# The scaling of the attention exponentials on GpSimd: one column as a second tensor in place of a number per partition

## The chip, the core and the metric

The kernel runs on one core of a Trainium2 chip. The metric is the device time of one execution in microseconds. Five engines take part: TensorE (PE in the profile; its weight loads PEld), VectorE (DVE), ScalarE (ACT), GpSimd (POOL) and SyncE (SP), which issues the DMAs. They run side by side and wait for each other by semaphores.

## What is computed

The program is a network of two blocks with two layers each, for 512 tokens of width 1024, with 256 context tokens beside them in the second block. The change lies in the attention of the second block's last layer:

```python
def gqa_sdpa(q, k, v):
    B, Q, H, Dh = q.shape
    qg = q.reshape(B, Q, N_KV_HEADS, KV_GROUP, Dh)
    s = jnp.einsum("bqkgd,bskd->bkgqs", qg, k).astype(jnp.float32) * (Dh ** -0.5)
    p = jax.nn.softmax(s, axis=-1).astype(v.dtype)
    o = jnp.einsum("bkgqs,bskd->bqkgd", p, v)
    return o.reshape(B, Q, H * Dh)
```

There are 16 heads of 64 and 4 heads of keys and values; 512 queries look at 512 + 256 = 768 keys. Behind the attention come its output product (wo), a norm and a gated feed-forward layer.

## The kernel before, in words

The attention is the function `gqa_attend` on TensorE, with loops over the same tiles on the other engines. A tile is one head and 128 queries, so there are 64 tiles n = 0 to 63, four to a head. Each tile goes through these steps:

- TensorE, `scores` (L1004, L1005): four matmuls write 128x768 scores into one of two pairs of PSUM banks. They wait for L2263 of tile n - 2.
- VectorE, L1802: reduction to the negative maximum.
- ScalarE, L2263: exponential into p2 (five buffers, 128x768 fp32 in SBUF), with the sum of each row in rs2. For an odd tile it also waits for the transposes of tile n - 5 and of the tile before that.
- VectorE, L1814: reciprocal of the sum into ri2, one column of a small tile.
- GpSimd, L2355: p2 = p2 x ri2, in place. This is the line that changes.
- TensorE, `turn`: transposes of p2 (L1015 four blocks of a tile, L1022 the two context blocks of both tiles of a pair, after the odd one).
- ScalarE, L2271 and L2275: the high part of the transposes; VectorE, L1819 and L1823: the low part.
- TensorE, `pv` (L1035, L1036): 12 matmuls for a pair of tiles, into the head's half of the PSUM bank of y2. All heads use the one bank of the ring "mod"; the first pair of a head waits until the head before is out of it.
- ScalarE, L2283, moves one half of y2 to SBUF (stat_t); VectorE, L1809, adds both halves into y2_out and frees the bank.
- For every second head ScalarE, L2287, and VectorE, L1828, split y2_out into a high and a low part in q_parts, which the output product reads. L1828 is the one large operation of VectorE here with two SBUF inputs.

Each engine works through its queue in the order in which it is written. In step n TensorE runs scores of n, then for even n the PV product of the pair (n - 8, n - 7), then the transposes of n - 4. VectorE runs in step n: L1802 of n; L1809 where n mod 4 is 3 (of head (n - 11)/4); L1814 of n - 1; L1819 of n - 5; L1823 for even n; L1828 where n mod 8 is 1. ScalarE runs L2263 of n, L2271 of n - 4, L2275 for odd n, and L2283 where n mod 4 is 2. GpSimd has nothing but L2355 in this stage, and waits before each for L1814 of the tile. Earlier in the program GpSimd takes the low parts of half of the weights (L2310, a subtraction with two full tensor inputs) and builds the weights of a convolution (L2327, a product whose second input repeats each value 32 times by a step of zero); in the attention TensorE's products need no weights from DMA.

Names: `sum_inverse` is the signal of L1814, `p2_scaled` that of L2355. P is 128, SEQ 512, CTX 256.

Of the kernel before, what the change touches and what calls it, by code (L numbers as in the profile page):

```python
# [17 lines left out]
ALU = mybir.AluOpType  # L18
# [6 lines left out]
P = 128  # L25
# [6 lines left out]
class Tally:  # L32
# [17 lines left out]
    def mark(self, name, *event, by=1):  # L50
        self.raised[name] = self.raised.get(name, 0) + by
        assert (name, event) not in self.at, (name, event)
        self.at[name, event] = self.raised[name]
        return self.sems[name], by

    def ready(self, name, *event):
        if self.known is None:
            return self.sems[name], self.at.get((name, event), 1)
        return self.sems[name], self.known[name, event]
# [34 lines left out]
def write(nc, a, out, tally):  # L94

    mark, ready = tally.mark, tally.ready
    _, SEQ, D = a["x"].shape
    CTX = a["ctx_2"].shape[1]
    DEPTH = a["w_in"].shape[0]
# [90 lines left out]
    def vec(name, i=0, n=1):  # L190
        c = vec_at[name] + i
        return vcols[:, c:c + n]

    def const(name, lo=0, n=None):
        c, w = CST[name]
        return cst[:, c + lo:c + (w if n is None else lo + n)]
# [76 lines left out]
    p2 = [nc.alloc_sbuf_tensor_at(f"p2{i}", [P, SEQ + CTX], F32, offset=int(hl_base + 8 * KB + 3 * KB * i)) for i in range(2)]  # L273
# [4 lines left out]
    ri2 = [small[:, 40 + i:41 + i] for i in range(5)]  # L278
# [15 lines left out]
    for row, n, src, dup in vec_rows:  # L294
        while n:
# [8 lines left out]
            row, n = row + k, n - k  # L304
# [13 lines left out]
    def full(job):  # L318
        return ready("bank_full%d" % bank_of[job], *job)

    def free(job):
        return tally.sems["bank_free%d" % bank_of[job]], use_of[job]
# [47 lines left out]
    def by_pool(key):  # L370

        return key[0] in BLOCK_1_SLABS or key[0:2] == ("dn", 1)
# [12 lines left out]
    def _(pe):  # L385
# [78 lines left out]
        def linear_pair_both(tag, *two):  # L464

            c_tag = (*tag[:-1], "c")
            hc = h_of(c_tag)
            tally.h_before[tag] = tally.h_before[c_tag] = tally.h_reader[0]
            ws = []
            for job, src, kind in two:  # L470
                begin(job, "pair")
                ws.append(slab(job, k_p(src), KD, src.shape[1], kind))
            tally.h_reader[0] = two[1][0]
            for s, t in (("x", tag), ("c", c_tag)):
                for i in range(KD):
                    pe.wait_ge(*ready("h_low", t, i))
                    for (job, _, _), w in zip(two, ws):
                        mm = both(job, w, i, slice(0, P), (Hh[:, i, :], Hl[:, i, :]), (hc[0][:, i, :], hc[1][:, i, :]),
                                  i == 0, i == KD - 1, s)
                        if s == "c" and i == KD - 1:  # L480
                            mm.then_inc(*fill(job))
                            release[job] = full(job)

        def linear_pair(tag, n, *two):

            tally.h_before[tag] = tally.h_reader[0]
            ws = []
            for job, src, kind in two:
                begin(job)
                ws.append(slab(job, k_p(src), KD, src.shape[1], kind))  # L490
            tally.h_reader[0] = two[1][0]
            for i in range(KD):
                pe.wait_ge(*ready("h_low", tag, i))
                for (job, _, _), w in zip(two, ws):
                    mm = three(bank(job, n), w[0][:, i, :], w[1][:, i, :], Hh[:, i, 0:n], Hl[:, i, 0:n],
                               i == 0, i == KD - 1)
                    if i == KD - 1:
                        mm.then_inc(*fill(job))
                        release[job] = full(job)
            mods()  # L500
            mods()
# [643 lines left out]
    def halves(slab, src, dst):  # L1145

        _, _, k, w, kind = slab
        if kind != "twice":
            return src[:, 0:k * w], dst[:, 0:k * w]
        return (src[:, 0:k * w].rearrange("p (k c) -> p k c", k=k).unsqueeze(2).broadcast_to([P, k, 2, w]),  # L1150
                dst[:, 0:2 * k * w].rearrange("p (k e c) -> p k e c", k=k, e=2))
# [1148 lines left out]
    @block.gpsimd  # L2300
    def _(pool):
        for i, (o, src) in enumerate(pieces[1]):
            pool.dma_start(o, src).then_inc(*mark("vec_in_rest", *([i] if i + 1 < len(pieces[1]) else []), by=16))
        for d, one in enumerate(slabs):
            if not by_pool(one[0]):
                break
            src, high = halves(one, raw[d % RAW], Wh[d % WS])
            _, low = halves(one, raw[d % RAW], Wl[d % WS])
            pool.wait_ge(*ready("w_high", one[0]))
            pool.tensor_tensor(low, src, high.bitcast(F32), ALU.subtract).then_inc(*mark("w_low_pool", one[0]))  # L2310


        w_dw = vec("w_dw", 0, TAPS * KD).rearrange("p (t j) -> p t j", j=KD)
        pool.wait_ge(*ready("w_low_pool", slabs[d - 1][0]))
        for g in range(4):
            for i in range(4):
                one = pool.tensor_copy(tap_cols[32 * i:32 * i + 32, g, :, :],
                                       w_dw[32 * g:32 * g + 32, PE_FIRST + i:PE_FIRST + i + 4 * QUADS - 3:4, :])
                one.then_inc(*mark("tap_cols", g, i))
                pool.wait_ge(*ready("tap_cols", g, i))  # L2320
        pool.wait_ge(*full(("dn", 1, DEPTH - 1, "x", 1, KD - 1)))
        for j in range(KD):
            if j >= 2:
                pool.wait_ge(*full(("taps", j - 2)))
            w = tap_cols[:, :, :, j].rearrange("p g q -> p q g").unsqueeze(3).broadcast_to([P, QUADS, 4, 32])
            fold = const("fold").unsqueeze(1).unsqueeze(1).broadcast_to([P, QUADS, 4, 32])
            pool.tensor_tensor(WQ[j % 2][:, :, :, :], fold, w, ALU.mult).then_inc(*mark("tap_weights", j))  # L2327

        def own(inst, *event):
            inst.then_inc(*mark("ctx_parts", *event))  # L2330
            return ready("ctx_parts", *event)

        pool.wait_ge(*ready("x_new", ("ffn", 0, "x"), KD - 1))
        pool.wait_ge(*ready("head_scaled", "k2", "c", KVH // 2 - 1))
        pool.wait_ge(*free(("turned", "v2", "c", 1)))
        for e in range(2):
            at_e = slice(e * HD, (e + 1) * HD)
            src = k_ctx[at_e, 0:KVH // 2, :]
            for d in range(2):
                pool.wait_ge(*own(pool.tensor_copy(k_hi[d * HD:(d + 1) * HD, e::2, SEQ:], src), "k", e, d))  # L2340
            for d in range(2):
                low = pool.tensor_tensor(k_lo[d * HD:(d + 1) * HD, e::2, SEQ:], src, k_hi[at_e, e::2, SEQ:].bitcast(F32),
                                         ALU.subtract)
                pool.wait_ge(*own(low, "k_low", e, d))
        for c in range(2):
            v = v_ctx[:, :, c * P:(c + 1) * P].rearrange("p t (g d) -> p t g d", g=2)
            one = v_parts[:, QT:, 2 * c:2 * c + 2, :, :]
            for b in (0, 2):
                pool.wait_ge(*own(pool.tensor_copy(one[:, :, :, b, :], v), "v", c, b))
            i = pool.tensor_tensor(one[:, :, :, 1, :], v, one[:, :, :, 0, :].bitcast(F32), ALU.subtract)  # L2350
        own(i)
        for n in range(G_HEADS * QT):
            h, i = divmod(n, QT)
            pool.wait_ge(*ready("sum_inverse", n))
            pool.tensor_scalar(p2[n % 5][:, :], p2[n % 5][:, :], ri2[n % 5], None, ALU.mult)\  # L2355
                .then_inc(*mark("p2_scaled", h, i))

    @block.sync
# [111 lines left out]
```

## Time and profile before

| | us |
|---|---|
| median of 3 runs | 3382.73 |
| lowest, highest | 3376.64, 3382.94 |
| the profiled execution | 3380.34 |
| its span, first to last instruction | 3378.5 |
| TensorE busy | 3250.6 (96%) |
| VectorE busy | 1484.0 (44%) |
| ScalarE busy | 1189.3 (35%) |
| GpSimd busy | 764.8 (23%) |

The mean granted clock of TensorE is 0.987 of full speed, and 1.00 in nearly all of the attention stage. The stage runs from about 2771 to 2919 us of the span. The shares are means over the whole program: GpSimd's 23% says nothing of the one stage in which it works without a pause. Matmuls are pipelined and the end of each is modelled, so times of TensorE are best read from start to start. A group in the list of groups gives busy time, mean length of one and the idle time before them, with what ended it.

### The profile page before, as it was taken

The numbers are of one execution on the slowest core, as the hardware profiler recorded it, in microseconds if no ns is written. First come the engines' busy times: TensorE is split into PE (matmuls) and PEld (weight loads), VectorE is DVE, ScalarE is ACT, GpSimd is POOL, SyncE is SP. The second block draws the span as 40 slices with busy tenths as digits, with TensorE's granted clock in tenths as the row PEclk, the third lists the DMA queues.
The fourth block names the chain that finished last, engine by engine and source line by source line (L and its number), as shares of the span: only waits on it lengthen the run. The fifth ranks groups of instructions, "written<-read, shape, count | busy, mean of one in ns | idle before, by whom it ended". The sixth has DMA issues, their size and how long they took to land.

```text
span 3378.5 us, 39102 instructions
## 1 busy us (share of the span) xinstructions
PE 3250.6 (96%) x15860; PEld 2490.3 (74%) x15860; DVE 1484.0 (44%) x2110; ACT 1189.3 (35%) x1752; POOL 764.8 (23%) x399
## 2 busy tenths in 40 slices
PE   6999999999998999999999899999999879999998
PEld 4657777777665776777777576888888648868886
DVE  3562143132356114313369746222334889653234
ACT  3433234233343323423331154111112558632222
POOL 4302433443330333434311000000000039500000
PEclk9999999999999999999999999999999989999999
DMA  6403434444440355455435311222221110123322
GB/s 231 139 26 94 150 118 149 151 142 151 124 126 19 117 158 168 149 188 161 133 88 128 83 47 39 65 63 64 68 63 57 38 38 1 38 69 89 104 85 72
DMA packets 429894, 337.25 MB, mean 100 GB/s; under 512 B 16637, under 2 KB 411223, under 8 KB 417428
## 3 DMA queue, kind: packets, MB, share of 16 engines
q1 hardware_dynamic: 428272, 334.23, 32.7%
q8 instruction: 127, 2.08, 0.3%
q0 software_dynamic: 1248, 0.46, 0.1%
q14 instruction: 51, 0.42, 0.0%
q10 hardware_dynamic: 196, 0.07, 0.0%
HBM read 319.58 MB, written 2.10 MB: 95 GB/s over the span
## 4 chain that ended last, share of the span: by engine, by line
PE 85%; DVE 6%; POOL 4%; ACT 2%; issue 1%; SPq 1%; DMA 0%; POOLq 0%; DVEq 0%; ACTq 0%
PE PS L422 25%; PE PS L423 24%; PE PS L424 24%; POOL p L2355 4%; PE PS L585 3%; PE PS L511 2%; PE PS L735 1%; PE PS L890 1%; PE PS L564 1%; PE PS L924 1%; SPq L2380 1%; DVE both_tmp L1260 1%; PE PS L943 1%; PE PS L901 1%; PE PS L923 1%
## 5 line engine op out<-in xcount | busy, mean ns | idle before, releaser
L422 PE MATMUL PS<-Hh,Wh 128*128 128x512 f32 x2208 | 876.9, 397 | 13.8 <-DVE Hl L1274 9.6
L423 PE MATMUL PS<-Hl,Wh 128*128 128x512 f32 x2208 | 862.8, 391 | 0.0
L424 PE MATMUL PS<-Hh,Wl 128*128 128x512 f32 x2208 | 862.3, 391 | 0.0
L2310 POOL TENSOR_TENSOR Wl<-raw,Wh 128x1024 fp32r<-128x1024 f32 (+2 forms) x254 | 568.3, 2242 | 1119.4 <-ACT Wh L1861 1119.4
L1861 ACT ACTIVATE Wh<-raw 128x1024 fp32r<-128x1024 f32 (+2 forms) x442 | 435.9, 987 | 402.9 <-PE PS L424 394.3
L422 PEld LDWEIGHTS PS<-Hh,Wh 128*128 128x128 f32 x2208 | 416.1, 188 | 138.2 <-issue 73.5
L424 PEld LDWEIGHTS PS<-Hh,Wl 128*128 128x128 f32 x2208 | 416.2, 189 | 87.8
L423 PEld LDWEIGHTS PS<-Hl,Wh 128*128 128x128 f32 x2208 | 416.3, 189 | 67.3 <-issue 3.1
L1183 DVE TENSOR_TENSOR Wl<-raw,Wh 128x1024 fp32r<-128x1024 f32 (+3 forms) x188 | 217.6, 1158 | 385.8 <-ACT Wh L1861 385.4
L1764 DVE SCALAR_TENSOR_TENSOR cv<-PS,vcols,cv 128x510 f32<-128x510 f32 (+1 forms) x176 | 123.7, 744 | 296.2 <-ACT cv L2231 296.2
L422 PE MATMUL PS<-g_h,Wh 128*128 128x512 f32 x528 | 210.6, 399 | 0.0
L423 PE MATMUL PS<-g_l,Wh 128*128 128x512 f32 x528 | 208.6, 395 | 0.0
L424 PE MATMUL PS<-g_h,Wl 128*128 128x512 f32 x528 | 208.5, 395 | 0.0
L2340 POOL CAST k_hi<-k_ctx 64x512 fp32r<-64x512 f32 x4 | 3.6, 912 | 815.4 <-DVE k_ctx L1260 815.2
L422 PE MATMUL PS<-hc_h,Wh 128*128 128x256 f32 x576 | 163.1, 283 | 1.0 <-DVE hc_l L1274 0.9
L423 PE MATMUL PS<-hc_l,Wh 128*128 128x256 f32 x576 | 161.9, 281 | 0.0
L424 PE MATMUL PS<-hc_h,Wl 128*128 128x256 f32 x576 | 161.8, 281 | 0.0
L2355 POOL TENSOR_SCALAR p<-p,small 128x768 f32<-128x768 f32 x64 | 141.7, 2237 | 56.2 <-DVE small L1814 56.2
L1738 DVE SCALAR_TENSOR_TENSOR X<-PS,mod,X 128x512 f32<-128x512 f32 x48 | 36.0, 751 | 261.0 <-PE PS L424 261.0
L511 PE MATMUL PS<-sq,cst 128*128 128x512 f32 (+2 forms) x244 | 114.4, 587 | 32.6 <-ACT sq L1896 13.6
L2231 ACT ACTIVATE cv<-PS,vcols 128x512 f32<-128x512 f32 x88 | 68.5, 778 | 211.7 <-PE PS L424 210.2
L422 PEld LDWEIGHTS PS<-g_h,Wh 128*128 128x128 f32 x528 | 99.1, 188 | 37.8 <-issue 14.7
(357 smaller groups left out, 4863.8 us busy)
## 6 DMA issues: line engine op xcount, KB each, us to landing
raw<-in_ffn_w SPq DMA_DIRECT2D x108, 512.0 KB, 3.7
mod_w<-in_w_mod SPq DMA_DIRECT2D x48, 1024.0 KB, 5.4
raw<-in_w_up SPq DMA_DIRECT2D x88, 512.0 KB, 3.8
mod_w<-in_w_ada SPq DMA_DIRECT2D x40, 1024.0 KB, 5.9
raw<-in_w_in SPq DMA_DIRECT2D x62, 512.0 KB, 4.1
UQ<-U SPq DMA_DIRECT2D x128, 99.4 KB, 2.2
raw<-in_w_down SPq DMA_DIRECT2D x32, 384.0 KB, 3.4
raw<-in_conv_w_pw SPq DMA_DIRECT2D x24, 512.0 KB, 4.5
```

What stands on the lines that cost most here:

```text
L422: pe.matmul(o, wh, xh, start=start, stop=False, skip_group_check=True)
L423: pe.matmul(o, wh, xl, start=False, stop=False, skip_group_check=True)
L424: return pe.matmul(o, wl, xh, start=False, stop=stop, skip_group_check=True)
L511: mm = pe.matmul(bank(job, n), const(matrix)[lo:hi, :], SQ[i][lo:hi, 0:n], start=first, stop=final, skip_group_check=True)
L585: mm = pe.matmul(PS[32 * j:32 * j + b, bank_of[job], :], cact[b][:, r, :], w[:, 512 * j:512 * (j + 1)], start=r == 0, stop=r == KD - 1, sk ...
L1183: dve.tensor_tensor(low, src, high.bitcast(F32), ALU.subtract).then_inc(*mark("w_low", k))
L1738: dve.scalar_tensor_tensor(X[:, j, :], bank(job), g, X[:, j, :], ALU.mult, ALU.add).then_inc(*empty(job))
L1764: ins = dve.scalar_tensor_tensor(o, bank(ups[s])[:, 0:SEQ - lag], vec(("w_conv", l), tap * 2 * FC + s * FC + f), o, ALU.mult, ALU.add)
L1861: act.activation(high, src, ACT.Copy).then_inc(*mark("w_high", k))
L2231: act.activation(cv[f % 2][s][:, :], bank(job), ACT.Identity, bias=vec(("b_conv", l), s * FC + f), scale=vec(("w_conv", l), 2 * 2 * FC + s ...
L2310: pool.tensor_tensor(low, src, high.bitcast(F32), ALU.subtract).then_inc(*mark("w_low_pool", one[0]))
L2355: pool.tensor_scalar(p2[n % 5][:, :], p2[n % 5][:, :], ri2[n % 5], None, ALU.mult)\
```

## The change

```diff
         for n in range(G_HEADS * QT):
             h, i = divmod(n, QT)
             pool.wait_ge(*ready("sum_inverse", n))
-            pool.tensor_scalar(p2[n % 5][:, :], p2[n % 5][:, :], ri2[n % 5], None, ALU.mult)\
+            pool.tensor_tensor(p2[n % 5][:, :], p2[n % 5][:, :], ri2[n % 5].broadcast_to([P, SEQ + CTX]), ALU.mult)\
                 .then_inc(*mark("p2_scaled", h, i))
```

GpSimd's 64 products take the reciprocal sums no longer as a number per partition but as a second tensor operand: the same column with a step of zero, read once for each of the 768 elements of a row. What is computed, the buffers, the waits and the order of all queues stay as they are.

## Rows read from the trace of the kernel before

**Rows 1.** The page: the span, and the chain that ended last.
```profile
span 3378.5 us, 39102 instructions
...
PE 85%; DVE 6%; POOL 4%; ACT 2%; issue 1%; SPq 1%; DMA 0%; POOLq 0%; DVEq 0%; ACTq 0%
```

**Rows 2.** The chain in order of time, 2760 to 2930: start, us, what.
```profile
2775.56 135.12 POOL p L2355 x61
```

**Rows 3.** A window amid the stage: length, busy PE, PEld, DVE, ACT, POOL, clock, DMA.
```profile
2820.00:2840.00 20.00, 19.55 (x147) 17.58 (x147) 19.24 (x37) 17.15 (x36) 20.00 (x10) 1.00 0.00 1
```

**Rows 4.** Waits from 2785 to 2905: who for whom, us in total, times, longest.
```profile
PE PS L1015 <- POOL p L2355: 2.2, 6, 0.4
PEld PS L1035 <- DVE y_out L1809: 1.7, 6, 0.3
```

**Rows 5.** Line L2355: duration in ns, shortest, median, longest, and where.
```profile
L2355 POOL TENSOR_SCALAR p<-p,small x64: 2198/2207/2535, 2772.9 to 2912.8; 128x768 f32<-128x768 f32 x64
```

**Rows 6.** Groups of GpSimd's instructions by shape: busy us, mean ns, idle before.
```profile
L2310 POOL TENSOR_TENSOR Wl<-raw,Wh 128x768 fp32r<-128x768 f32 x36 | 66.3, 1843 | 131.3 <-ACT Wh L1861 131.3
```

**Rows 7.** Instructions in time, GpSimd's L2327, then one of VectorE: start, us, what.
```profile
1718.08 2.13 POOL L2327 TENSOR_TENSOR WQ<-cst,tap_cols 128x512 f32<-128x512 f32 x2 [4.63 <-PE PS L424]
...
1795.86 2.63 POOL L2327 TENSOR_TENSOR WQ<-cst,tap_cols 128x512 f32<-128x512 f32 x1 [20.66 <-PE PS L735]
...
2805.89 0.68 DVE L1828 TENSOR_TENSOR q_parts<-y_out,q_parts 128x512 fp32r<-128x512 f32 x1
```

**Rows 8.** TensorE in order of time, amid the stage.
```profile
2792.61 0.36 PE L1035 MATMUL PS<-pt_hi,v_parts 128*128 128x256 f32 x1
...
2799.41 0.28 PE L1005 MATMUL PS<-k_lo,q_parts 128*128 128x256 f32 x1
...
2801.47 0.39 PE L1035 MATMUL PS<-pt_hi,v_parts 128*128 128x256 f32 x1
...
2802.99 0.60 PE L1015 MATMUL PS<-cst,p 128*128 128x128 f32 x4
2803.34 0.47 PE L1004 MATMUL PS<-k_hi,q_parts 128*128 128x512 f32 x1
...
2805.70 0.28 PE L1035 MATMUL PS<-pt_hi,v_parts 128*128 128x256 f32 x1
...
2808.14 0.28 PE L1005 MATMUL PS<-k_lo,q_parts 128*128 128x256 f32 x1
...
2810.39 0.33 PE L1035 MATMUL PS<-pt_hi,v_parts 128*128 128x256 f32 x1
```

**Rows 9.** VectorE in order of time, the same stretch.
```profile
2799.73 0.96 DVE L1802 TENSOR_REDUCE small<-PS 128x1 f32<-128x768 f32 x1 [0.35 <-PE PS L1005]
2800.72 0.69 DVE L1809 TENSOR_TENSOR y_out<-PS,stat_t 64x512 f32<-64x512 f32 x1
...
2803.18 0.67 DVE L1819 TENSOR_TENSOR pt_lo<-PS,pt_hi 128x512 fp32r<-128x512 f32 x1
2803.77 0.68 DVE L1823 TENSOR_TENSOR pt_lo<-PS,pt_hi 128x512 fp32r<-128x512 f32 x1
...
2808.61 0.94 DVE L1802 TENSOR_REDUCE small<-PS 128x1 f32<-128x768 f32 x1
2809.60 0.68 DVE L1809 TENSOR_TENSOR y_out<-PS,stat_t 64x512 f32<-64x512 f32 x1
```

**Rows 10.** The stage's end: four rows of TensorE, then one of VectorE.
```profile
2908.20 0.39 PE L1035 MATMUL PS<-pt_hi,v_parts 128*128 128x256 f32 x1 [0.68 <-DVE y_out L1809]
...
2909.73 0.60 PE L1015 MATMUL PS<-cst,p 128*128 128x128 f32 x4
2910.82 0.63 PE L1015 MATMUL PS<-cst,p 128*128 128x128 f32 x4 [0.49 <-POOL p L2355]
...
2917.92 0.35 PE L1035 MATMUL PS<-pt_hi,v_parts 128*128 128x256 f32 x1 [0.25 <-DVE pt_lo L1823]
...
2915.03 0.68 DVE L1809 TENSOR_TENSOR y_out<-PS,stat_t 64x512 f32<-64x512 f32 x1 [1.54 <-ACT stat_t L2283]
```

## The prediction

> **What bounds the kernel now.** I read the page first. The span is 3378.5 us, and the time of this execution is 3380.34, so 1.84 us lie outside it; sums below are made on 3380.34. The chain of work that ended last is 85% TensorE and 4% GpSimd, and those 4% are one line, L2355, the one that changes [rows 1]. In order of time, that share is one unbroken piece: GpSimd carries the chain from 2775.56 for 135.12 us, all of it the scaling of the exponentials in the last attention [rows 2]. So the change touches 64 instructions in one stage of about 147 us, and that stage's end decides, since the gemm behind it starts as soon as it ends.
>
> That GpSimd is the bound there is only half of the story. In the middle of the stage GpSimd is busy all of 20 us, but TensorE 19.55 and VectorE 19.24 [rows 3]. Three engines run nearly full, so a faster GpSimd gives only what lies between its pace and the next. The waits say which is next: from 2785 to 2905 TensorE waited 2.2 us for the scaling, and 1.7 us in six places for VectorE's addition L1809 to release a PSUM bank [rows 4].
>
> **What the change costs by itself.** Removed: 64 TENSOR_SCALAR of 128x768, shortest 2198 ns, median 2207 [rows 5]. Added: 64 TENSOR_TENSOR of 128x768, whose second input is one column, with step zero. Waits, signals, buffers and the order on each queue stay the same. The trace of before has no TENSOR_TENSOR with a one-column input of this length, so I bound it. With two full inputs and the same width GpSimd takes 1843 ns [rows 6]. Nearest with a step of zero is L2327 (512 wide; one input repeats each value 32 times): two of them take 2.13 us together, so about 1.07 each; alongside dense VectorE work on two SBUF tensors it takes 2.63 [rows 7]. Scaled by width these are 1.07 x 1.5 = 1.60 and 2.63 x 1.5 = 3.95. I take 1.84: same width, same memory, two inputs. The 3.95 is an end for the bad case only, because in this stage VectorE's big operations read PSUM and at most one SBUF tensor; only L1828, eight times, reads two. One of those starts at 2805.89 [rows 7] in the middle of a scaling; the longest scaling, 2535 ns, is the mark of it [rows 5], +0.33 us.
>
> The Trainium skill ("GPSIMD Engine Reference", section 4.1) says that two-input elementwise operations are about 2x slower on GpSimd than on VectorE while one-input ones run roughly at line rate; by that the swap would be a loss. The trace says otherwise: the one-input form takes 2207 ns for 768, the two-input form 1843. The Trainium skill's own figure for a two-input add (the same page, section 3.1, 4497 ns for 2048 elements) would make 768 an estimated 1.69 us; the sum below would not move by it.
>
> **What is late next.** GpSimd alone would save 64 x (2.21 - 1.84) = 24 us. It can't, since another circuit closes almost as tightly. The PV products of all heads (4 tiles each) share one PSUM bank, which L1809 frees. L1809 stands on VectorE's queue right behind a reduction L1802; that reduction waits for its tile's scores; those scores stand on TensorE's queue behind the first PV product of the head that holds the bank now; and the next head's first PV product waits for this L1809. Step by step, from rows in which no wait for GpSimd lies:
> - TensorE from L1035 at 2801.47 to the last score matmul at 2808.14: 6.67 us [rows 8] (two PV products, three groups of scores, and the transposes between).
> - last score matmul to the reduction: 2799.41 to 2799.73, 0.32 us where VectorE is free; 2808.14 to 2808.61, 0.47, where it is still busy with the L1828 of that head pair [rows 8, 9].
> - reduction to L1809: 2799.73 to 2800.72, and 2808.61 to 2809.60: 0.99 both times; L1809 itself 0.69; its end to L1035 0.06 (2801.41 to 2801.47) [rows 8, 9].
> Sum: 6.67 + 0.32 + 0.99 + 0.69 + 0.06 = 8.73 us for four tiles. Every second head has L1828, and there VectorE has no gap at all from L1809 at 2800.72 to L1809 at 2809.60, 8.88 us [rows 9]; with L1809 and 0.06 behind it that gives the next L1035 at 2810.34, where it now stands at 2810.39 [rows 8]: 8.87. The pair costs 8.73 + 8.87 = 17.60 us.
>
> Today: from L1035 at 2792.61 to L1035 at 2908.20 are 13 intervals, 115.59 us, mean 8.89 [rows 8, 10]. The kind with L1828 (2801.47 to 2810.39) is 8.92, the other kind (115.59 - 6 x 8.92) / 7 = 8.87, by the rows one by one 8.86. So the gain in the steady part is 7 x (8.86 - 8.73) + 6 x (8.92 - 8.87) = 0.9 + 0.3 = **1.2 us**. Before 2792.61 nothing is gained: that first L1035 already waits for an L1809 (its own reduction waits for TensorE, not for GpSimd).
>
> The drain. GpSimd is two tiles behind there, and that backlog vanishes. Transposes 61 start at 2910.82 after a wait for GpSimd; they follow the group at 2909.73, and such a group holds TensorE 0.35 (2802.99 to 2803.34 [rows 8]), so they could start at 2910.08, 0.74 earlier. Everything to L1809 at 2915.03 (PV, transposes 62, ScalarE's copy) moves with them, to 2914.29. The scaling of tile 63 no longer queues behind others and is done well before. Then VectorE runs L1809, two L1819 and L1823 back to back, 0.59 apart (2803.18 to 2803.77 [rows 9]), the last one for its 0.68, and TensorE takes it up about 0.15 later: 2914.29 + 3 x 0.59 + 0.68 + 0.15 = 2916.9 for the last L1035, now 2917.92 [rows 10]: **1.0 us**. Behind it TensorE runs the same gemms, shifted.
>
> Sum: 3380.34 - 1.2 - 1.0 = 3378.1, say **3378.0 us**, 0.07% less. The median of the runs shown, 3382.73, is 2.4 us above the profiled one; from there it would be 3380.5. A change of under 0.2% (6.8 us) can hardly be told from none with runs that spread over 6.3 us.
>
> The GpSimd price doesn't enter this, as long as it stays under the circuit: eight scalings and one +0.33 must fit in 17.60, so up to (17.60 - 0.33) / 8 = 2.16 us. Both 1.60 and 1.84 give the same time. That is the cover, and it is thin on the other side: from 2.16 up each 0.1 us costs 6.4.
>
> **The rivals.**
> - The circuit is looser than I think (L1809 follows its reduction sooner, as VectorE catches up), and TensorE's own work sets the pace. From L1035 at 2801.47 to the next tile pair's at 2805.70 are 4.23 us [rows 8], 4.13 without the 0.10 by which the waiting L1035 runs long, so 8.26 for four tiles: 13 x (8.89 - 8.26) + 1.0 = 9.2 us gained: 3371.1. Against it: 0.99 stands at both places shown, and waits of L1035 for L1809 exist already [rows 4]. Chance 0.10.
> - The other side: the one-column input is slow. If the same column read 768 times costs what L2327 costs beside a busy VectorE, 3.95 us, GpSimd sets the pace: 63 x (3.95 - 2.21) = 110 us more, 3490. It decides from 2.16 us; at 2.54 (the longest scaling today) it is 63 x 0.33 = 21 us, 3401. Against it: L2327 with a step of zero takes 1.07 when it is left alone. Chance 0.06. The Trainium skill's rule above, taken at its word (section 4.1, a one-input form at twice the rate), would end here too: an estimated 4.4 us each and some 3519.
> - L1828 gets blocked behind a scaling. Six of the eight lie in the tight heads; each blocked for a whole 1.84 us is 11 us more on VectorE's unbroken chain, net 3389. Against it: L1828 takes 0.68 while a scaling runs [rows 7], as long as L1809 and L1819 of the same width [rows 9]; GpSimd stretches instead. Chance 0.03. "SBUF — State Buffer", section "SBUF: two separate sides", of the Trainium skill calls the shared port pair an exclusive lock for the whole instruction, whoever starts first; in the trace VectorE isn't held.
> - The change doesn't do what it says: the instruction ends up as the same one, 2.207 us. 3380.3. Chance 0.04.
>
> **How the numbers follow.** Forecast 0.77, the rivals 0.10, 0.06, 0.03, 0.04. Faster by over 0.2%: the looser circuit, 0.10. Slower by over 0.2%: 0.09. Within 0.2%: 0.77 + 0.04 = 0.81. The forecast's own range: the steady part can give between nothing and twice my 1.2, the drain between nothing and 1.0, and the runs shown lie 3.7 below to 2.6 above the profiled one; that makes 3373 to 3383. Widened to take in most of the looser circuit and the low end of the blocked L1828: **3370 to 3386**.
>
> **What would show it.** L2355 as TENSOR_TENSOR, at 1.6 to 1.85 us, and GpSimd idle before each one, waiting for L1814; its share in the chain gone from 4% to nearly nothing, DVE and PE in its place. L1035 waiting for L1809 in 13 places instead of 6 or 7, with intervals of 8.73 and 8.87. TensorE no longer waiting for GpSimd. The stage ending 2 us sooner. It would be wrong if L2355 took over 2.16 us, if the intervals fell well under 8.7, or if L1802, L1819 or L1828 grew longer beside the new operation.

## The result

The changed kernel takes 3387.95 us (median of 12 runs, 3383.65 to 3388.92); the kernel before takes 3382.2 in 12 runs beside it. The ratio is 1.0018, with a 95% interval of 1.0010 to 1.0027: slower by 3 to 9 us. The forecast was 3378.0, in a range of 3370 to 3386. The measured time lies above the range. What turned the gain of the attention stage into a loss is one of the forecast's own rivals, which it had given a chance of 0.03; that accounts for some 5 of the 10 us of the miss, and the section on the prediction says what the rest is.

The page of the kernel after: the span, the chain that ended last by engine, and then, from the list of GpSimd's groups by shape, the line that was changed.

```profile
span 3387.1 us, 39102 instructions
...
PE 87%; DVE 7%; ACT 2%; issue 2%; SPq 1%; DMA 0%; DVEq 0%; ACTq 0%
...
L2355 POOL TENSOR_TENSOR p<-p,small 128x768 f32<-128x768 f32 x64 | 93.8, 1468 | 104.5 <-DVE small L1814 103.2
```

GpSimd has left the chain altogether (4% in [rows 1]), its scaling is 0.74 us shorter than before (1468 ns against a median of 2207 [rows 5]), and it now stands idle for 104.5 us waiting for reciprocals, 55.7 of them before its first scaling (before the change 56.2 in all). Two thirds of the old price, and the kernel is slower. The waits of the kernel after from 2771 to 2930, longest in total first:

```profile
POOL p L2355 <- DVE small L1814: 103.2, 45, 55.7
...
PEld PS L1035 <- DVE y_out L1809: 9.1, 15, 1.1
```

TensorE's wait for L1809 is the one that grew: from 2771 to 2918 in the kernel before it was 2.6 us in 7 places. Where it comes from shows in VectorE's queue around the line L1828, then GpSimd's at the same time (start, us, what):

```profile
2810.45 0.67 DVE L1819 TENSOR_TENSOR pt_lo<-PS,pt_hi 128x512 fp32r<-128x512 f32 x1
2811.04 1.59 DVE L1828 TENSOR_TENSOR q_parts<-y_out,q_parts 128x512 fp32r<-128x512 f32 x1
2812.55 0.94 DVE L1802 TENSOR_REDUCE small<-PS 128x1 f32<-128x768 f32 x1
...
2810.61 1.47 POOL L2355 TENSOR_TENSOR p<-p,small 128x768 f32<-128x768 f32 x1 [0.65 <-DVE small L1814]
```

L1828 takes 1.59 us; before it took 0.68 [rows 7]. It starts 0.43 us after a scaling has started and ends 0.55 after that scaling's end (2810.61 + 1.47 = 2812.08): it was held. Over all eight of its instances in the kernel after, shortest, median, longest:

```profile
L1828 DVE TENSOR_TENSOR q_parts<-y_out,q_parts x8: 681/1586/1592, 2811.0 to 2930.1; 128x512 fp32r<-128x512 f32 x8
```

Six take 1.59 us. The last two, at 2921.05 and 2930.07, start when no scaling is under way and take 0.68 and 0.69.

The first PV products of the heads, TensorE in order of time, give the pace:

```profile
2797.89 0.38 PE L1035 MATMUL PS<-pt_hi,v_parts 128*128 128x256 f32 x1
...
2806.61 0.38 PE L1035 MATMUL PS<-pt_hi,v_parts 128*128 128x256 f32 x1 [0.20 <-DVE y_out L1809]
...
2816.40 0.39 PE L1035 MATMUL PS<-pt_hi,v_parts 128*128 128x256 f32 x1 [0.23 <-DVE y_out L1809]
...
2825.14 0.39 PE L1035 MATMUL PS<-pt_hi,v_parts 128*128 128x256 f32 x1 [0.20 <-DVE y_out L1809]
...
2917.66 0.39 PE L1035 MATMUL PS<-pt_hi,v_parts 128*128 128x256 f32 x1 [0.90 <-DVE y_out L1809]
...
2926.41 0.35 PE L1035 MATMUL PS<-pt_hi,v_parts 128*128 128x256 f32 x1 [0.20 <-DVE pt_lo L1823]
...
2927.85 0.39 PE L422 MATMUL PS<-q_parts,Wh 128*128 128x512 f32 x1
```

Intervals are 8.72, 9.79, 8.74 and so on in turn. Heads without L1828 run at the forecast 8.73 (8.86 before); heads with it at 9.79 (8.92 before, 8.87 forecast). From 2797.89 to 2917.66 are 119.77 us, before 115.59 [rows 8, 10]: 4.2 lost. From there to the first gemm behind are 10.19, before 11.20 (2908.20 to 2919.40): 1.0 won, as forecast. The stage costs 130.0 us in place of 126.8, **3.2 us more**.

The two profiled spans differ by 8.6 us, and 5.3 of these lie before the stage: L1035 at 2792.61 [rows 8] is L1035 at 2797.89 here. The change touches nothing there: the first scores of the stage (L1004) start at 2763.72 before and at 2769.01 now, 5.29 apart. What differs is where TensorE's granted clock was at its lower level (1.2 GHz for 3 to 17 us at a time, else 2.4). Two windows, from 220 to 235 and from 1050 to 1065 us, in the kernel before and then in the kernel after (length, busy PE, PEld, DVE, ACT, POOL, clock, DMA):

```profile
220.00:235.00 15.00, 11.37 (x51) 8.02 (x51) 8.84 (x11) 7.37 (x6) 0.00 (x0) 1.00 0.00 1
...
1050.00:1065.00 15.00, 11.37 (x42) 7.55 (x41) 9.46 (x11) 5.92 (x6) 0.00 (x0) 0.77 0.00 1
```

```profile
220.00:235.00 15.00, 11.37 (x42) 7.69 (x41) 8.66 (x9) 6.89 (x6) 0.00 (x0) 0.77 0.01 1
...
1050.00:1065.00 15.00, 11.37 (x54) 7.95 (x53) 10.58 (x13) 7.47 (x8) 0.00 (x0) 1.00 0.01 1
```

The same matmuls meet another clock, and not always to the loss of the same kernel. Up to the first scores the lower level lasted 69.9 us in all in the kernel before and 83.5 in the kernel after. ScalarE's instructions, matched between the two traces, show the lag grow by some 2.8 us after the low stretch at 224 and by 1.5 after the one at 914, and shrink by 2.8 where only the kernel before has one, at 1055. A comparison of two spans alone would have put 8.6 us down to the change; stages must be compared with stages.

### The profile page after: what moved, and what is told of

Its sections match the earlier page's. It is cut to its first block, busy times and chain, and to the rows that moved or that the text cites. A ratio compares the mean times of both kernels' runs of the same rounds, so it can differ in the third digit from the quotient of the medians.

```text
span 3387.1 us, 39102 instructions
## 1 busy us (share of the span) xinstructions
PE 3254.4 (96%) x15860; PEld 2491.2 (74%) x15860; DVE 1488.5 (44%) x2110; ACT 1189.9 (35%) x1752; POOL 717.4 (21%) x399
## 4 chain that ended last, share of the span: by engine, by line
PE 87%; DVE 7%; ACT 2%; issue 2%; SPq 1%; DMA 0%; DVEq 0%; ACTq 0%
PE PS L422 25%; PE PS L423 24%; PE PS L424 24%; PE PS L585 3%; PE PS L511 2%; PE PS L735 1%; PE PS L890 1%; PE PS L564 1%; PE PS L924 1%; SPq L2380 1%; DVE both_tmp L1260 1%; PE PS L943 1%; DVE small L1802 1%; PE PS L901 1%; PE PS L923 1%
## 5 line engine op out<-in xcount | busy, mean ns | idle before, releaser
L1183 DVE TENSOR_TENSOR Wl<-raw,Wh 128x1024 fp32r<-128x1024 f32 (+3 forms) x188 | 217.6, 1158 | 386.1 <-ACT Wh L1861 385.6
L422 PEld LDWEIGHTS PS<-hc_h,Wh 128*128 128x128 f32 x576 | 108.1, 188 | 23.8 <-DVE hc_l L1312 1.9
```

Of the source, the lines that this page charges most:

```text
L422: pe.matmul(o, wh, xh, start=start, stop=False, skip_group_check=True)
L1183: dve.tensor_tensor(low, src, high.bitcast(F32), ALU.subtract).then_inc(*mark("w_low", k))
```

## The experiments

All lengths of the stage below are from the first PV product of the second head (the row at 2792.61 in [rows 8]) to the first gemm behind the attention.

| kernel | scaling | stage, us | median, us (runs) | ratio to before |
|---|---|---|---|---|
| before | number | 126.8 | 3382.2 (12) | |
| changed | column | 130.0 | 3387.95 (12) | 1.0018 [1.0010, 1.0027] |
| again | column | 130.0 | 3387.93 (11) | 1.0016 [1.0007, 1.0025] |
| after_move | column | 125.3 | 3378.67 (11) | 0.9993 [0.9984, 1.0001] |
| before_move | number | 125.5 | 3383.0 (11) | 1.0003 [0.9994, 1.0011] |
| full2 | full tensor | 132.4 | 3389.72 (6) | 1.0025 [1.0014, 1.0036] |
| full2_move | full tensor | 125.7 | 3382.82 (10) | 1.0000 [0.9991, 1.0009] |
| yadd_first | column | 136.6 | 3395.37 (4) | 1.0043 [1.0027, 1.0058] |
| copy_first | column | 128.9 | 3384.89 (11) | 1.0007 [0.9998, 1.0016] |
| ts_copy_first | number | 129.2 | 3385.64 (11) | 1.0013 [1.0004, 1.0022] |
| pv_late | column | 134.1 | 3393.78 (5) | 1.0035 [1.0021, 1.0048] |
| ts_pv_late | number | 134.2 | 3393.09 (11) | 1.0029 [1.0020, 1.0037] |

The ratios are to the executions of the kernel before that ran beside each, with medians of 3381.5 to 3382.3.

The mean granted clock of an execution, from 0.985 to 0.989 on record, goes with the time whatever the kernel: a straight line with the same slope for each kernel, through the 174 executions of this table and of the kernel before beside them, gives an estimated 2.4 us for each 0.001. At equal clock the changed kernel (23 executions) lies 4.3 us above before (71), give or take 0.6 (95%); after_move lies 0.6 below and before_move 0.1 above, both give or take 0.8. The medians of the table mix such executions: seven of 71 of the kernel before had 0.988 or more, none of the 23 of the changed kernel, and four of the 11 of after_move.

### Is it the stage, always?

> The changed kernel as it is, once more, to see what of the 8.6 us between the two profiled spans belongs to the attention stage. 5.3 us of them lie before the stage, in places that the change does not touch, where the granted clock was at its lower level in other stretches. Theory: the stage itself costs 3.2 us, always (intervals of L1035 of 9.78 and 8.73 us in turn, L1828 1.59 us), and the 5.3 us upstream move from run to run; the median is 3 to 4 us above that of before. Rival: the upstream part is there in every run of this kernel, and its median lies 6 to 9 us above before.

Measured: L1828 at a median of 1590 ns, intervals of 8.73 and 9.79, the stage 130.04 us. The stage part of the theory holds. The median is again 5.6 us above that of before, between what the two expected. The 3.2 us of the stage are shown; some 2.5 more in the median aren't explained by it. In this run too the window from 220 to 235 had a clock of 0.77 and the attention began late. Over all kernels of the table the median less the stage lies between 3253 and 3260 us, without regard to the form of the scaling. At equal clock the 4.3 us leave 1.1 (give or take 0.6) beside the stage's 3.2, so about half of the 2.5 goes with the clock. Why the changed kernel had no execution at the higher clock, and the last 1.1 us, stay open.

### Does the order decide, or the form?

In the next two kernels L1828 moves ahead of the reciprocal L1814 of its step. With the new scaling it then starts while GpSimd waits:

```diff
+            if n >= 17 and n % 8 == 1:
+                j = (n - 17) // 8
+                dve.wait_ge(*ready("y2_high", j))
+                dve.tensor_tensor(y2_l[:, j, :], y2_out[:, :], y2_h[:, j, :].bitcast(F32), ALU.subtract)\
+                   .then_inc(*mark("y2_low", j))
             if 0 <= n - 1 < len(tiles):
                 dve.wait_ge(*free(("s2", *tiles[n - 1])))
...
-            if n >= 17 and n % 8 == 1:
-                j = (n - 17) // 8
...
```

> The changed kernel, and L1828 stands on VectorE's queue ahead of L1814 of its step instead of behind L1819, so that it starts while GpSimd is idle and has its answer before the next scaling can start. Theory of the shared port (of L1828, with two SBUF inputs, and a scaling, whichever comes second waits until the first is done): L1828 0.68 us instead of 1.59, the interval with L1828 8.73 to 8.9 instead of 9.78, the stage 5 to 6 us shorter than in the changed kernel, and some 2 us shorter than before. Rival (the tensor_tensor on GpSimd slows VectorE's two-input operations in general, or the new operation makes the step longer for another reason): L1828 stays over 1.2 us and the interval near 9.8.

Measured, L1828 (here L1813; L1814 is L1819 here) in this kernel, shortest, median, longest, and one of them beside the scaling that follows it:

```profile
L1813 DVE TENSOR_TENSOR q_parts<-y_out,q_parts x8: 691/693/695, 2810.0 to 2924.9; 128x512 fp32r<-128x512 f32 x8
```

```profile
2809.96 0.69 DVE L1813 TENSOR_TENSOR q_parts<-y_out,q_parts 128x512 fp32r<-128x512 f32 x1
...
2810.81 1.47 POOL L2355 TENSOR_TENSOR p<-p,small 128x768 f32<-128x768 f32 x1 [1.29 <-DVE small L1819]
```

0.69 us, all eight; intervals 8.73 and 8.92; the stage 125.3 us, 4.7 shorter than in the changed kernel (expected 5 to 6) and 1.5 shorter than before (expected some 2). In the stage the collision is the whole loss, and without it the forecast's circuit is what is left: 1.5 us won where 2.2 were forecast. The heads give 1.0 of 1.2, and the drain 0.5 of 1.0, since the moved L1828 waits there for ScalarE's high part, 1.19 us at 2915.38. The median falls by 9.3 against the changed kernel, twice what the stage gives; at equal clock it is 4.9, and the stage's 4.7 account for it. Against before the medians give 3.6 us with an interval that touches 1, and equal clock gives 0.6, give or take 0.8: the stage is shorter, but this kernel as a whole isn't shown to be faster than before.

> The kernel before, TENSOR_SCALAR, with the same move of L1828 ahead of L1814. GpSimd is always amid a scaling at that point (2803.90 to 2806.11, L1828 would come at 2805.23). Theory (order decides, the form of the scaling does not): L1828 now comes second and waits out the scaling, 1.2 to 2.2 us instead of 0.68; the scaling is no longer stretched to 2.53; the stage gets 0 to 5 us longer. Rival (it is the form: only TENSOR_TENSOR holds VectorE up, TENSOR_SCALAR never does): L1828 stays at 0.68 us and the scalings stretch to 2.53 as before, with the stage within 1 us of before.

Measured, the same line and an instance of it beside GpSimd's row (three scalings merged, from 2806.12; in the trace the second starts at 2808.30):

```profile
L1813 DVE TENSOR_TENSOR q_parts<-y_out,q_parts x8: 692/693/764, 2809.0 to 2924.1; 128x512 fp32r<-128x512 f32 x8
```

```profile
2809.00 0.76 DVE L1813 TENSOR_TENSOR q_parts<-y_out,q_parts 128x512 fp32r<-128x512 f32 x1
...
2806.12 6.59 POOL L2355 TENSOR_SCALAR p<-p,small 128x768 f32<-128x768 f32 x3
```

The theory (order alone decides) fell: seven of the eight L1828 came second, 0.7 to 1.4 us into a scaling, and weren't held, but for 0.07 us in the one that came soonest (the eighth comes after the last scaling). The rival (TENSOR_SCALAR never holds) didn't fit either: the scalings weren't stretched to 2.53 us, the longest is 2.25. The stage became 1.3 us shorter, which neither expected: two heads now take 17.65 us in place of 17.79. With the order the same, number and column differ by 0.2 us in the stage (125.5 and 125.3), so of the 1.5 us that after_move wins, the move alone gives 1.3. New theory: both forms hold the port, TENSOR_SCALAR only in its first part.

### How long does each form hold VectorE?

First a full second tensor in the changed kernel (this kernel's output isn't the reference's), then a small kernel with little but the two operations. The first edit, against the changed kernel:

```diff
-            pool.tensor_tensor(p2[n % 5][:, :], p2[n % 5][:, :], ri2[n % 5].broadcast_to([P, SEQ + CTX]), ALU.mult)\
+            pool.tensor_tensor(p2[n % 5][:, :], p2[n % 5][:, :], X[:, :, :].rearrange("p k n -> p (k n)")[:, 0:SEQ + CTX], ALU.mult)\
```

> The changed kernel, but the second input of the scaling is a full tensor of 128x768 in SBUF (the residual X) instead of the one column, so the attention's output is not the reference's. By L2310 such an operation takes 1.84 us, 0.37 more than the 1.468 of the one-column form. Theory (L1828 waits until the scaling that is under way has ended): L1828 starts 0.43 us into a scaling as now and ends 0.55 after it, so it grows by the same 0.37 to 1.96 us, the interval with L1828 to 10.15, the stage by 6 x 0.37 = 2.2 us. Rival (both share the port and slow each other by a factor): L1828 stays near 1.6, and the scaling beside it is longer than the rest.

Measured, L1828 and the scaling over the kernel, shortest, median, longest:

```profile
L1828 DVE TENSOR_TENSOR q_parts<-y_out,q_parts x8: 691/1978/1984, 2809.4 to 2930.8; 128x512 fp32r<-128x512 f32 x8
...
L2355 POOL TENSOR_TENSOR p<-p,X x64: 1815/1849/1880, 2775.3 to 2920.4; 128x768 f32<-128x768 f32 x64
```

The expectation was 1.96 us for L1828; the interval is 10.18 (10.15), the stage 132.4 (130.0 + 2.2 = 132.2). No scaling is stretched. The slowdown is no factor; L1828 waits for the scaling's end.

> A small kernel of its own that measures the disputed cost by itself (its output is not the reference's, it leaves out the whole network): 39 times VectorE sends a signal that starts a scaling of 128x768 on GpSimd, then runs a filler that reads PSUM alone (16 to 2048 wide, some 0.06 to 2.1 us), then a 128x512 subtraction with two SBUF inputs like L1828. 13 offsets for each of three scalings: a number per partition, one column as a tensor, a full tensor. Theory now, after the two moves of L1828: a tensor_tensor holds the second read port until it ends, so the subtraction always ends about 0.55 us after it, wherever it started; TENSOR_SCALAR holds the port only in its first 0.8 us of 2.2 (the one L1828 that started 0.70 into a scaling took 0.76, those from 0.94 on 0.69), so only offsets under 0.8 us are held, and they end near 1.3 after the scaling's start. Rival: TENSOR_SCALAR never holds VectorE up, at any offset (0.69 throughout), and is itself stretched where the subtraction came first. Second rival: what decides is who starts first in both forms, and a scaling under way holds the subtraction to its end in all three (then the 0.69 of the moved L1828 would stay unexplained).

VectorE's part of the small kernel, for each filler width w:

```python
dve.tensor_reduce(red[:, 0:1], PS[:, 0:512], AX.X, ALU.min).then_inc(s["go"], 1)
dve.tensor_reduce(red[:, 1:2], PS[:, 0:w], AX.X, ALU.min)
dve.tensor_tensor(yl[:, :], yo[:, :], yh[:, :].bitcast(F32), ALU.subtract).then_inc(s["dve"], 1)
```
It ran once. Four offsets with TENSOR_SCALAR, first the scalings and then the subtractions that belong to them:

```profile
11.05 2.71 POOL L49 TENSOR_SCALAR p<-p,col 128x768 f32<-128x768 f32 x1 [0.82 <-DVE red L37]
14.58 2.20 POOL L49 TENSOR_SCALAR p<-p,col 128x768 f32<-128x768 f32 x1 [0.82 <-DVE red L37]
...
26.68 2.21 POOL L49 TENSOR_SCALAR p<-p,col 128x768 f32<-128x768 f32 x1 [0.82 <-DVE red L37]
29.70 2.20 POOL L49 TENSOR_SCALAR p<-p,col 128x768 f32<-128x768 f32 x1 [0.82 <-DVE red L37]
```

```profile
11.07 0.70 DVE L39 TENSOR_TENSOR yl<-yo,yh 128x512 fp32r<-128x512 f32 x1
14.74 1.29 DVE L39 TENSOR_TENSOR yl<-yo,yh 128x512 fp32r<-128x512 f32 x1
...
27.37 0.75 DVE L39 TENSOR_TENSOR yl<-yo,yh 128x512 fp32r<-128x512 f32 x1
30.52 0.68 DVE L39 TENSOR_TENSOR yl<-yo,yh 128x512 fp32r<-128x512 f32 x1
```

And with the column as a second tensor, three offsets:

```profile
51.47 1.47 POOL L51 TENSOR_TENSOR p<-p,col 128x768 f32<-128x768 f32 x1 [0.80 <-DVE red L37]
60.13 1.47 POOL L51 TENSOR_TENSOR p<-p,col 128x768 f32<-128x768 f32 x1 [1.42 <-DVE red L37]
...
74.57 1.47 POOL L51 TENSOR_TENSOR p<-p,col 128x768 f32<-128x768 f32 x1 [1.42 <-DVE red L37]
```

```profile
51.50 1.98 DVE L39 TENSOR_TENSOR yl<-yo,yh 128x512 fp32r<-128x512 f32 x1
...
60.56 1.58 DVE L39 TENSOR_TENSOR yl<-yo,yh 128x512 fp32r<-128x512 f32 x1
...
75.80 0.78 DVE L39 TENSOR_TENSOR yl<-yo,yh 128x512 fp32r<-128x512 f32 x1
```

Add start and length, and take off the scaling's start. TENSOR_SCALAR: 14.74 + 1.29 - 14.58 = 1.45; 27.37 + 0.75 - 26.68 = 1.44; from 0.82 us of offset on (30.52 - 29.70), 0.68 without a hold. Unheld it takes 0.68, so it is let in 0.76 us after the scaling's start, of 2.20. The column: 51.50 + 1.98 - 51.47 = 2.01, 2.01 at 60.56 and 2.01 at 75.80, 0.55 behind the scaling's end at all nine offsets from 0.03 to 1.24 us: let in at 1.33 of 1.47. The full tensor gave the same with 1.80: ends 0.55 behind it at all ten offsets from 0.04 to 1.50 us. Where the subtraction comes first or in the same moment (11.07), it isn't held and the scaling is stretched, to 2.56 and 2.71 us for the number, 1.92 for the column, 2.26 for the full tensor. The theory holds in both parts; both rivals fall.

The hold by TENSOR_SCALAR shows in a kernel of the next section too, ts_copy_first, one of two places there:

```profile
2919.85 2.21 POOL L2355 TENSOR_SCALAR p<-p,small 128x768 f32<-128x768 f32 x1
```

```profile
2920.43 0.87 DVE L1813 TENSOR_TENSOR q_parts<-y_out,q_parts 128x512 fp32r<-128x512 f32 x1 [0.21 <-ACT q_parts L2287]
```

2920.43 + 0.87 - 2919.85 = 1.45, as in the small kernel. In the other the subtraction starts at 2829.37, 0.24 after the scaling, takes 1.20 and ends 1.44 after the scaling's start.

> L1828 moved ahead of L1814, and the scaling with a full second tensor (the residual X, so the output is not the reference's), 1.80 to 1.85 us in place of 1.47. With the collision gone, the theory says that the scaling's price is wholly hidden behind the circuit of y2's bank: intervals 8.73 and 8.92 as with the one-column form, the stage 125.3 us within 0.5. Rival: the scaling's price counts after all (0.37 us x 64 = 24 us if it were on the path, or 2 us and more in part), or L1828 still collides.

Measured: scalings of 1848 ns, intervals 8.73 and 8.92, the stage 125.7. L1828 is at 0.69 in seven of eight; the eighth, in the drain, takes 1.12 and ends 0.54 after the scaling beside it. 0.38 us more in each of 64 scalings leaves the steady part where it was (114.57 against 114.63 us) and the stage within 0.4, all of it in the drain: the price is hidden, as long as nothing collides. Where it does, the price counts through the hold: full2's stage is 2.4 us longer than the changed kernel's.

### Can the circuit of y2's bank be loosened?

> The changed kernel with L1828 moved, and L1809 ahead of the reduction L1802 of its step on VectorE. If the circuit through the one PSUM bank of y2 sets the pace (intervals 8.73 and 8.92), taking L1802 out of it helps only as far as ScalarE's copy L2283 is there: it ends 0.25 and 0.04 us before L1809 starts in the kernel before, so intervals of 8.5 and 8.9, the stage 1 to 2 us shorter than with L1828 moved alone. Rival: VectorE's own load is the bound, and the swap changes nothing or costs up to 3 us, since the reduction and with it the exponential come 0.6 us later.

> As the last one, and on ScalarE L2283 also stands ahead of L2271 of its step, so that L1809 has its input 0.5 us earlier. If the circuit is the bound, the intervals fall to what TensorE needs for its own work, 8.3 to 8.5 us, and the stage is 5 to 7 us shorter than with L1828 moved alone (some 119 to 120 us from the first PV product to the first gemm behind, against 125.3). Rival: something else holds at 8.7, and the stage stays within 1 us.

> The same order of the queues with the scaling of before, TENSOR_SCALAR with a number per partition. If the circuit is what hid the faster scaling, then with the circuit loosened GpSimd is the bound here: eight scalings of 2.21 us make 17.7 us for two heads, intervals of 8.8 on average, and 13 x (8.85 - 8.4) + 1 = 5 to 7 us more than with the one-column tensor_tensor in the same order. Rival: the two forms are within 1 us of each other in this order too.

The edits, on VectorE and then, for the last two, on ScalarE:

```diff
+            if 11 <= n < len(tiles) + 8 and n % QT == 3:
...
+                dve.tensor_tensor(y2_out[rows, :], bank(("y2", h))[rows, :], ST[rows, :], ALU.add).then_inc(*empty(("y2", h)))
             if n < len(tiles):
                 job = ("s2", *tiles[n])
...
-            if 11 <= n < len(tiles) + 8 and n % QT == 3:
...
```

```diff
+            if 10 <= n < len(tiles) + 7 and n % QT == 2:
...
+                act.activation(ST[rows, :], bank(("y2", h))[other, :], ACT.Copy).then_inc(*mark("y2_other", h))
             if 0 <= n - 4 < len(tiles):
                 job, u = ("pt2", *tiles[n - 4]), (n - 4) // 2
...
-            if 10 <= n < len(tiles) + 7 and n % QT == 2:
...
```

L1828 stands ahead of L1814 in all kernels from here on; ts_copy_first and ts_pv_late have the TENSOR_SCALAR line of before.

Measured: stages of 136.6, 128.9 and 129.2, all longer than 125.3. Intervals are 9.28 and 9.98 in yadd_first, about 8.9 and 9.4 in copy_first. VectorE's wait for ScalarE's copy from 2790 to 2912, in yadd_first and then in copy_first (L1803 is L1809 here, and in copy_first L2271 is L2283):

```profile
DVE y_out L1803 <- ACT stat_t L2283: 13.7, 13, 1.2
```

```profile
DVE y_out L1803 <- ACT stat_t L2271: 7.4, 13, 0.7
```

VectorE, which had no time to lose, now waits for ScalarE's copy 13 times in each, and every reduction behind it comes later, with its exponential. The rival of yadd_first had the mechanism, but 3 us at most for 11.3. In copy_first the expected gain of 5 to 7 us was wrong: TensorE no longer appears in the waits for L1809 in copy_first, but the intervals grew all the same: the bound is now on VectorE's side. The two forms of the scaling differ by 0.3 us: neither is the bound there, so the rival held, and the expected 5 to 7 us between them weren't to be seen.

> The one-column scaling, L1828 moved, and on TensorE the first PV product of each head, which waits for L1809, comes behind the transposes of its step instead of ahead of them. If the circuit of y2's bank is the bound, it loses the 0.35 us of these transposes: 8.38 for the heads without L1828; with L1828 VectorE's own chain holds at 8.7 to 8.9. Pairs of 17.1 to 17.3 us instead of 17.65, the stage 2 to 3.5 us shorter than the 125.3 of L1828 moved alone. Rival: VectorE or the reductions hold everything at 8.7, no gain.

> The same with TENSOR_SCALAR. With the circuit at 17.1 to 17.3 us for two heads, eight scalings of 2.208, 17.66, are the bound: intervals of 8.83 on average, GpSimd without a pause, and the stage 2 to 4 us longer than with the one-column tensor_tensor in the same order. Rival: no difference, within 0.5 us.

The edit, on TensorE:

```diff
-                if n >= 8 and n % 2 == 0:
+                if n >= 8 and n % 4 == 2:
                     pv((n - 8) // 2)
                 if 0 <= n - 4 < len(tiles):
                     turn(n - 4, *tiles[n - 4])
+                if n >= 8 and n % 4 == 0:
+                    pv((n - 8) // 2)
```

Measured: 134.1 and 134.2, intervals 9.46 and 9.60. Both expectations fell; the rival of the second, no difference, held. The transposes, now first, meet a wait that the PV product had covered: their bank is freed by L1819 of tile n - 6, which stands behind L1809 on VectorE. TensorE at such a place (L1826 is L1819 here), one of 12 with 11.9 us in all:

```profile
2846.58 0.66 PE L1015 MATMUL PS<-cst,p 128*128 128x128 f32 x4 [1.12 <-DVE pt_lo L1826]
```

So of the orders tried only the move of L1828 shortened the stage. In the others a wait at another place grew, VectorE's for ScalarE's copy or TensorE's for L1819, and the stage got 3.6 to 11.3 us longer than 125.3. Whether some other order does better isn't shown.

## Why the prediction was wrong

- The price of the new operation: 1.84 was taken, between 1.60 and 3.95; measured 1.468. The row with a step of zero, scaled, was nearer than the row of the same width. "The GpSimd price doesn't enter this" is right only where nothing collides, as full2_move shows. In the changed kernel it enters through the hold; 1.84 would have cost some 2.4 us more (full2, with 1.85).
- The Trainium skill's rule on one and two inputs ("GPSIMD Engine Reference", section 4.1) pointed the wrong way for these operations: one input 2.20, two inputs 1.47 and 1.80 us at 768. The Trainium skill's own figure for two inputs (the same page, section 3.1) gave an estimated 1.69, against 1.80 here.
- The circuit through y2's bank: forecast 8.73 for heads without L1828, measured 8.68 to 8.74. It is now what TensorE waits for. This step was right, and so was the drain: forecast 1.0, measured 1.0 (from the last head's first L1035 to the last L1035 forecast 8.72, here 2926.41 - 2917.66 = 8.75).
- **The step that failed** is the reading of one row. The forecast has L1828 at 2805.89 "in the middle of a scaling", and from that "L1828 takes 0.68 while a scaling runs" against the rival that it gets blocked. Beside the new scaling it takes 1.59. GpSimd's row of the kernel before over this time merges two scalings:

```profile
2803.93 4.72 POOL L2355 TENSOR_SCALAR p<-p,small 128x768 f32<-128x768 f32 x2
```

It ends at 2803.93 + 4.72 = 2808.65, and the second of the two is the stretched one, of 2.535 [rows 5], so that one starts at 2806.11, 0.22 us after L1828. L1828 came in the last 0.25 us of the first scaling, when by the measurement above TENSOR_SCALAR has long let go, and ahead of the second, which was made to wait. The row showed who wins when VectorE is first; it was taken to show that VectorE is never held. The 0.33 us on that scaling was the trace's sign that the two do collide. The trace of before also had VectorE held by a TENSOR_TENSOR, beside the very L2327 at 1795.86 whose 2.63 us the forecast took for its bad case [rows 7]. VectorE at that time; L1381 and L1183 have two inputs in SBUF:

```profile
1795.39 1.03 DVE L1381 SCALAR_TENSOR_TENSOR both_tmp<-U,vcols,both_tmp 128x783 f32<-128x783 f32 x1
1796.34 1.22 DVE L1183 TENSOR_TENSOR Wl<-raw,Wh 128x1024 fp32r<-128x1024 f32 x1
1797.47 1.86 DVE L1381 SCALAR_TENSOR_TENSOR CV<-U,vcols,CV 128x783 f32<-128x783 f32 x1
```

L2327 starts 0.47 us after the first of these L1381 and ends at 1798.49. By its unheld 1.07 us it began its work at 1797.42, 0.14 before the end of L1183, which had followed without a gap: two VectorE operations in a row kept it out. The second L1381 starts within that work, takes 1.86 us in place of 1.03 and ends 0.84 after L2327. Of 104 L1381 in that kernel five take 1.86, all beside such an L2327; the other 99 take 1.02 to 1.03. That VectorE can lose the time, and not only GpSimd, was there to be read.
- With L1828 held, the heads with it take 9.79 us in place of 8.92. Six of these lie in the stretch: 5.14 us lost, 0.96 won in the seven others, 1.01 in the drain; 3.2 in all. The rival had a whole 1.84 us for each, 11 in all, and 3389; the hold is 0.91, because L1828 starts 0.43 into a scaling of 1.47. That its 3389 lies within 1 us of the measured median is luck: its mechanism is right, its price twice too high. Had it been given its weight, the range would have reached to 3389.
- The rule of the Trainium skill ("SBUF — State Buffer", section "SBUF: two separate sides"), an exclusive lock for the whole instruction to whoever starts first, was set aside with "VectorE isn't held". The runs agree with it for TENSOR_TENSOR, up to the last 0.14 us, and for VectorE first; they don't for TENSOR_SCALAR, which lets VectorE in after 0.76 of 2.20 us. That difference is what the change brought in: in the kernel before the seventh L1828, at 2911.60, started 0.95 us into a scaling and took 0.68 all the same.
- The forecast counted two circuits that VectorE's queue is part of, but costed only waits by semaphores. A hold at a port is in no list of waits; it shows as a longer instruction. The forecast named that sign ("or if L1802, L1819 or L1828 grew longer"), and it is where the answer stood.
- The size of the miss, 9.9 us, in parts: 5.4 are the stage, forecast at -2.2 and measured at +3.2; 1.9 are the start from the profiled execution at 3380.34 in place of the median of 3382.2; 2.5 are the rest of the program, of which about half goes with the granted clock and half stays open. With the stage alone, 3380.3 + 3.2 = 3383.5 or 3382.2 + 3.2 = 3385.4, the time would have been within the range. So the failed step decides the sign, and that the time fell outside the range it does together with a rest that no run explains in full.

## What to carry to other kernels

A faster operation on GpSimd can cost VectorE more than it gives: ask what it holds while it runs, and look for the VectorE operations with two SBUF inputs on a tight queue. To see whether two operations collide, read their starts one by one; a merged row, or the length of one of the two alone, can't tell who was first. Where they do, put VectorE's ahead of the signal that starts GpSimd's, and measure that move without the faster operation too: here the move alone gave 1.3 us of the stage's 1.5. Before two medians are compared, look at the granted clock of the executions behind them.

## What the runs showed of the hardware

- A scaling of 128x768 fp32 in SBUF on GpSimd takes 2.20 us with a number per partition, 1.47 with that column as a second tensor of step zero, 1.80 to 1.85 with a full second tensor.
- While it runs it keeps a VectorE operation with two inputs in SBUF out for the first 0.76 us (number), 1.33 (column) and 1.66 (full tensor), for the last two its length less 0.14. Why the number's hold is so much shorter than its 2.20 us stays open.
- VectorE's operation with one input in PSUM and one in SBUF isn't held by either form: L1819 has a mean of 673 ns in the kernel before and 674 after, and its longest is 692 in both.
- If VectorE's is first, GpSimd's is stretched by 0.33 us in the attention (2.535 for 2.207), up to 0.5 when both start in the same moment (2.71). Where VectorE's was clearly first, the stretch is the time from GpSimd's start to VectorE's end, less 0.13 to 0.14: 0.49 and 0.36 for the number, 0.60 and 0.46 for both tensor forms in the small kernel, 0.46 and 0.33 in the attention.
- The granted clock's low stretches don't fall in the same places in every execution of the same instructions: 71 executions of the kernel before had mean clocks from 0.985 to 0.989 and times from 3375.5 to 3386.0, the shorter ones at the higher clock.
